# A Conformer and mixture-of-experts layer: the residual in token layout, the first norm by diagonal matrices, modulation rows spread through DRAM

## What is computed

```python
mod = silu(c) @ ada_w + ada_b
sh1, sc1, g1, sh2, sc2, g2 = split(mod, 6)
h = rmsnorm(x, mix_norm_g) * (1 + sc1) + sh1
u = h @ pw1_w + pw1_b                      # 2048 columns
a, gt = split(u, 2);  u = a * sigmoid(gt)
u = causal_depthwise_conv(u, dw_w, dw_b)   # 31 taps
u = silu(layernorm(u, ln_g, ln_b))
x = x + g1 * (u @ pw2_w + pw2_b)
h = rmsnorm(x, ffn_norm_g) * (1 + sc2) + sh2
logits = h @ router_w + router_b           # 32 experts, the best 4 of each token
gate = softmax(top 4 logits)
x = x + g2 * sum over the 4 of gate * expert(h)   # 1024 -> 2048, clamped SwiGLU, 1024 -> 1024
out = rmsnorm(x, final_norm_g)
```

## Time and profile before

| what | value |
|---|---|
| median of 3 runs | 1175.99 us (1170.95 to 1177.86) |
| the profiled execution's own time | 1175.84 us |
| its span, first to last instruction | 1174.0 us |
| TensorE busy | 994.6 us (85%) |
| VectorE busy | 354.4 us (30%) |
| ScalarE busy | 163.5 us (14%) |
| read from HBM | 455.79 MB, 389 GB/s over the span |
| TensorE's mean granted clock | 0.942 |

### The profile page before, as it was taken

One profiled execution on the slowest core, in us unless ns is written; L12 is line 12 of the kernel. 1 busy time (PEld: TensorE's weight loads), 2 busy tenths in 40 slices (PEclk: granted clock), 3 DMA queues, 4 the chain that ended last, 5 costly groups with the idle time before them and its releaser, 6 DMA issues.

```text
span 1174.0 us, 21008 instructions
## 1 busy us (share of the span) xinstructions
PE 994.6 (85%) x7636; PEld 468.4 (40%) x7637; DVE 354.4 (30%) x952; ACT 163.5 (14%) x360; POOL 8.1 (1%) x21
## 2 busy tenths in 40 slices
PE   5999988898999787999887999887899887878755
PEld 3776663334443333444323344323444322332322
DVE  3788555221222222132222123212112322222222
ACT  2333252101001101011110011010111010101002
POOL 1000000000000000000000000000000000000000
PEclk9999997998989998989998989998989989898978
DMA  9985964999999999999999999999999999999995
GB/s 356 285 346 190 392 247 172 420 421 421 422 372 424 422 422 422 421 392 424 422 422 422 422 417 399 421 422 421 423 421 392 422 422 422 422 422 422 422 421 228
DMA packets 84441, 457.24 MB, mean 389 GB/s; under 512 B 9183, under 2 KB 29783, under 8 KB 30622
## 3 DMA queue, kind: packets, MB, share of 16 engines
q1 hardware_dynamic: 83088, 456.16, 95.6%
q10 hardware_dynamic: 1326, 0.71, 0.2%
HBM read 455.79 MB, written 1.05 MB: 389 GB/s over the span
## 4 chain that ended last, share of the span: by engine, by line
PE 52%; DMA 34%; SPq 5%; DVE 4%; issue 3%; ACT 1%; ACTq 1%; POOL 0%; DVEq 0%; POOLq 0%
DMA ring<-in_exp_w 34%; PE bank L1252 22%; PE bank L1275 11%; PE bank L1124 5%; SPq L298 5%; PE bank L1145 2%; PE bank L1231 2%; PE bank L1072 2%; PE bank L1108 1%; PE bank L1219 1%; PE bank L1229 1%; PE bank L1262 1%; PE bank L1243 1%; DVE scratch L904 1%; PE bank L1054 1%
## 5 line engine op out<-in xcount | busy, mean ns | idle before, releaser
L1252 PE MATMUL bank<-ring,xg 128*32 128x256 f32 (+2 forms) x3200 | 443.8, 481 | 58.9 <-DMA ring<-in_exp_w 58.4
L1252 PEld LDWEIGHTS bank<-ring,xg 128*32 128x32 f32 (+2 forms) x3200 | 168.0, 129 | 320.7 <-issue 175.6
L1275 PE MATMUL bank<-ring,actT 128*32 128x512 f32 (+2 forms) x1056 | 217.2, 615 | 22.7 <-DMA ring<-in_exp_w 14.6
L531 ACT ACTIVATE act<-scratch 128x128 f32<-128x128 f32 (+2 forms) x66 | 25.6, 388 | 766.3 <-DVE scratch L904 764.9
L1275 PEld LDWEIGHTS bank<-ring,actT 128*32 128x32 f32 (+2 forms) x1056 | 75.5, 133 | 140.4 <-issue 109.0
L904 DVE TENSOR_SCALAR scratch<-bank 128x128 f32<-128x128 f32 (+2 forms) x66 | 25.3, 384 | 312.6 <-PE bank L1252 312.6
L893 DVE SCALAR_TENSOR_TENSOR acc<-bank,gate,acc 128x512 f32<-128x512 f32 x136 | 93.0, 743 | 54.7 <-PE bank L1231 45.4
L923 DVE TENSOR_TENSOR ysb<-bank,g2half 128x512 f32<-128x512 f32 x29 | 20.1, 692 | 219.0 <-PE bank L1275 219.0
L1219 PEld LDWEIGHTS bank<-onehot_bf,arena 128*128 128x128 bf16 x1632 | 57.4, 102 | 23.0 <-issue 23.0
L1231 PE MATMUL bank<-ysb,onehotT 64*128 64x512 f32 x240 | 60.4, 615 | 2.9 <-DVE ysb L923 2.1
L1219 PE MATMUL bank<-onehot_bf,arena 128*128 128x32 bf16 (+2 forms) x1632 | 61.0, 195 | 1.0 <-DVE arena L833 1.0
(11 more groups left out here) (222 smaller groups left out, 515.2 us busy)
## 6 DMA issues: line engine op xcount, KB each, us to landing
ring<-in_exp_w SPq DMA_DIRECT2D x396, 1024.0 KB, 24.1
ring<-in_ada_w SPq DMA_DIRECT2D x24, 1024.0 KB, 10.2
ring<-in_conf_pw_w SPq DMA_DIRECT2D x12, 1024.0 KB, 11.9
acc<-in_x SPq DMA_DIRECT2D x1, 1024.0 KB, 4.9
out<-acc SPq DMA_DIRECT2D x2, 512.0 KB, 3.1
g2full<-in_ada_b SPq DMA_DIRECT2D x1, 512.0 KB, 4.3
xT<-in_final_norm_g ACTq DMA_DIRECT2D x1, 512.0 KB, 3.7
b1f<-in_exp_b SPq DMA_DIRECT2D x1, 256.0 KB, 3.7
```

What stands on the lines that cost most here:

```text
L531: a.activation(act[:, h * c:(h + 1) * c], g_lim[h][:, 0:c], ACT.Sigmoid, scale=ALPHA).then_inc(sig_ready, 1)
L1252: ins = mm(up_to(m, n, r), xg[:, b, k, 0:m], wk[:, at:at + span(m)], start=False, stop=(k == KT - 1))
L1275: ins = mm(dst, actT[:, f % (2 * q), at:at + m], wk[:, f % 2 * D + r * H:f % 2 * D + (r + 1) * H], start=(f < sides), stop=(f >= KT - sides))
```

## The change

- The residual stays in `acc`, tokens as rows, all the way; `xT`, the turns of x2 and of h, and `pick` go.
- First norm: ScalarE sums the squares of each row, VectorE scales the identity by 1/rms of each token into two diagonal matrices, and x is turned by a product with them.
- Modulation columns: the stream begins with four chunks that hold only the scale columns (two blocks of 128 rows in each), then the first pw1 tile, then four chunks of shift columns, then the other pw1 tiles. Tile 0 is multiplied with scaled columns that have no shift yet; its bias is corrected by shift times weight, which TensorE makes as a row and turns in the middle of tile 1.
- pw2 goes with tokens as rows and 1024 outputs in two halves: token tile 0 over all channels, then the halves of token tile 1; a chunk holds 256 rows of pw2_w in pieces of 4 KB.
- g1, sh2, the second scale times norm gain (`a2_row`), g2 and g1 times the bias of pw2 are needed as rows on all 128 partitions. Each is stored to a DRAM scratch (`keep`) and read back into all partitions (`spread`). The first three spreads stand ahead of expert 0 on SyncE's queue, the last two behind its eighth chunk.
- Router: its weights are scaled by a2 and multiplied with turned x2, the shift's logits are one row (`log_row`), the norm is applied to the logits. Second norm: sums of squares by ScalarE in halves.
- Token tile 0 is routed and split while tile 1 is in work. The splitting of the expert biases moves in part to ScalarE; GpSimd no longer splits. `g2full` comes from DRAM; `ysb` and `gate4` are prepared behind the selection. The 13 transfers of convolution weights are issued behind the scale row. Rows of `ada_b`, `ffn_g` and `pw2_b` are loaded in 12 pieces with the small tensors, behind the twelfth chunk.

The core of the diff:

```diff
-    stream = [("ada", k) for k in range(KT)]
-    for t in range(KT):
+    stream = [("scale", q) for q in range(4)] + [("pw1", 0)] + [("shift", q) for q in range(4)]
+    for t in range(1, KT):
...
+                    two = slice(2 * k * P, (2 * k + 2) * P)
+                    src = (pw2_w[0, two, :] if what == "pw2" else
+                           ada_w[0, two, D:2 * D] if what == "scale" else ada_w[0, two, 0:D]
+                           ).rearrange("(a p) n -> p a n", p=P)
...
+            def keep(g):
+                sp.dma_start(mod_rows[g][0:2 * D].rearrange("(j n) -> j n", j=4),
+                             modrow[g][bass.ds(0, 4, 32), :]).then_inc(s_kept, 16)
+            def spread(to, g, at, landing):
+                sp.dma_start(to, mod_rows[g][at:at + D].partition_broadcast(P)).then_inc(landing, 16)
+            sp.wait_ge(s_row, 3)
+            keep(0)
+            sp.wait_ge(s_gbias, 1)
+            sp.dma_start(mod_rows[0][2 * D:3 * D].rearrange("(j n) -> j n", j=2),
+                         gbias_row[bass.ds(0, 2, 32), :]).then_inc(s_kept, 16)
+            sp.wait_ge(s_kept, 32)
+            spread(g1_row, 0, 0, s_rows1)
+            spread(xb_row, 0, 2 * D, s_rows1)
+            spread(sh2_row, 0, D, s_rows1)
...
+                    if first and q == KT - 1:
+                        sp.wait_ge(s_row, 4)
+                        keep(1)
+                        sp.wait_ge(s_kept, 48)
+                        spread(a2_row, 1, 0, s_rows2)
+                        spread(g2full[:, :], 1, D, s_rows2)
+            expert(0, 0, True)
...
+            a.wait_ge(p_c, 1)
+            a.activation(cact[:, :], bank[1][:, 0:KT], ACT.Silu).then_inc(s_cact, 1)
+            a.wait_ge(s_x, 16)
+            for t in range(TT):
+                a.activation(flat[:, t * D:(t + 1) * D], acc[:, t, :], ACT.Square,
+                             accum_out=ssq[:, t:t + 1]).then_inc(s_sq, 1)
+            a.wait_ge(s_const_v, 1)
+            a.wait_ge(s_sq, TT)
+            a.activation(fin[:, :], ssq[:, :], ACT.Sqrt, scale=1.0 / D, bias=eps[:, 0:1]).then_inc(s_fr0, 1)
+            a.wait_ge(p_vec, 1)
+            a.activation(vcol[:, :], bank[0][:, 0:VECS], ACT.Copy).then_inc(v_vec, 1)
+            a.wait_ge(used, number["scale", 3] + 1)
+            a.activation(modrow[0], bank[7][:, :], ACT.Copy).then_inc(s_row, 1)
...
+            a.wait_ge(p_sh, 1)
+            a.activation(modrow[1], bank[7][:, :], ACT.Copy).then_inc(s_row, 1)
+            a.wait_ge(used, number["shift", 3] + 1)
+            a.activation(crow, bank[0][:, T:2 * T], ACT.Copy).then_inc(s_crow, 1)
...
+                if t == 0:
+                    a.wait_ge(s_fix, 1)
...
+            squared(0, 0)
+            squared(0, 1)
+            rooted(0)
+            x2T_out(0, 0, 5)
+            x2T_out(0, 1, 6)
+            high(0, 0)
+            high(0, 1)
+            mid(0, 0)
+            mid(0, 1)
+            squared(1, 0)
+            x2T_out(1, 0, 1)
+            squared(1, 1)
+            rooted(1)
+            x2T_out(1, 1, 2)
+            high(1, 0)
+            high(1, 1)
...
+            v.wait_ge(s_fr0, 1)
+            link(v.reciprocal(frstd[:, :], fin[:, :]))
+            for t in range(TT):
+                v.tensor_scalar(diag[:, t, :], ident[:, :], frstd[:, t:t + 1], None, ALU.mult).then_inc(s_diag, 1)
...
+                v.tensor_scalar(hT[:, k, :], normed(k), a1[:, k:k + 1], None, ALU.mult).then_inc(s_h, 1)
...
+            v.wait_ge(p_row, 2)
+            column(sh1, P + KT, AB)
+            v.wait_ge(s_mod, 2)
+            v.tensor_copy(sh1wide, sh1[:, :].unsqueeze(2).to_broadcast([P, KT, 32])).then_inc(s_sw, 1)
+            v.wait_ge(p_t0, 1)
+            for k in range(KT):
+                v.tensor_scalar(hT[:, k, :], normed(k), a1[:, k:k + 1], sh1[:, k:k + 1],
...
+            v.wait_ge(p_corr, 1)
+            v.tensor_tensor(vcol[:, bass.ds(PB1, 2, 8)], bank[0][:, P + 16:P + 18], vcol[:, bass.ds(PB1, 2, 8)],
+                            ALU.add).then_inc(s_fix, 1)
+            v.wait_ge(s_fix, 1)
...
+            v.wait_ge(s_ab, 16 * 12)
+            v.wait_ge(used, number["ada", 2 * KT - 1] + 1)
+            v.tensor_tensor(modrow[0], bank[6][:, :], ada_rows[0], ALU.add).then_inc(s_row, 1)
...
+            v.tensor_tensor(gbias_row, modrow[0][0:64, :], pw2b_row, ALU.mult).then_inc(s_gbias, 1)
+            v.wait_ge(used, number["ada", 3 * KT - 1] + 1)
+            link(v.tensor_tensor(modrow[1], bank[7][:, :], ada_rows[1], ALU.add))
+            v.scalar_tensor_tensor(out=modrow[1][0:64, :], in0=modrow[1][0:64, :], scalar=1.0, in1=ffng_row[:, :],
+                                   op0=ALU.add, op1=ALU.mult).then_inc(s_row, 1)
...
+            v.wait_ge(s_rows1, 48)
+            for t in range(TT):
+                step(v.tensor_tensor(acc[:, t, :], acc[:, t, :], xb_row, ALU.add))
...
+            v.wait_ge(p_lrow, 1)
+            link(v.tensor_tensor(log_row[:, :], bank[0][:, 3 * P:3 * P + E], rb_row[:, :], ALU.add))
...
+            v.wait_ge(p_y, 1)
+            done = [gated_y(0, r) for r in range(2)]
             for r in range(2):
+                residual(0, r, done[r])
+            v.wait_ge(s_rows2, 32)
+            for r in range(2):
+                scaled(0, r)
+            base(0)
+            normed2(0)
+            for r in range(2):
+                modulated(0, r)
+            for r in range(2):
+                rest_of(0, r)
+            v.wait_ge(p_y, 2)
+            residual(1, 0, gated_y(1, 0))
+            scaled(1, 0)
+            logits(0)
+            choose(0)
+            for r in range(2):
+                low(0, r)
             for r in range(2):
                 step(v.tensor_copy(g2half[64 * r:64 * r + 64, :], g2full[64 * r:64 * r + 64, r * H:(r + 1) * H]))
+            base(1)
+            v.wait_ge(used, CH_EXP)
+            residual(1, 1, gated_y(1, 1))
+            scaled(1, 1)
+            normed2(1)
+            modulated(1, 0)
+            modulated(1, 1)
+            logits(1)
+            choose(1)
+            rest_of(1, 0)
...
+            low(1, 0)
+            low(1, 1)
+            step(v.scalar_tensor_tensor(out=key[:, :], in0=counts, scalar=float(E), in1=tie[:, :],
+                                        op0=ALU.mult, op1=ALU.add))
+            step(v.tensor_scalar(over[:, :], counts, float(WIDE), None, ALU.is_gt))
+            step(v.tensor_scalar(over2[:, :], counts, float(WIDE + SMALL), None, ALU.is_gt))
+            v.wait_ge(s_b2, 32)
+            v.tensor_tensor(ysb[:, 0, :], b2f[:, :], g2half[:, :], ALU.mult).then_inc(y_ready, 1)
+            step(v.memset(gate4, 0.0))
...
+            half_row("scale", 0).then_inc(used, 1)
+            pe.wait_ge(s_diag, TT)
             for k in range(KT):
                 for t in range(TT):
...
+                    ins = mm(bank[3 + k // 2][:, (k % 2) * T + t * P:(k % 2) * T + (t + 1) * P],
+                             acc[:, t, k * P:(k + 1) * P], diag[:, t, :], start=True, stop=True)
+            ins.then_inc(p_x, 1)
...
+            pe.wait_ge(*chunk_in(number["pw1", 0]))
+            pw1_half(0, 0)
+            pw1_half(0, 1).then_inc(p_t0, 1)
+            for q in range(4):
+                ins = half_row("shift", q)
+            ins.then_inc(p_sh, 1)
...
+                if t == 1:
+                    pe.wait_ge(s_crow, 1)
+                    for h in range(2):
+                        ins = mm(bank[0][:, P + 16 + h:P + 17 + h], crow[:, h * P:(h + 1) * P], sel1[:, :],
+                                 start=True, stop=True)
+                    ins.then_inc(p_corr, 1)
+                pw1_half(t, 1).then_inc(used, 1)
+                taps(t - 1)
...
+            for k in range(KT):
+                if k % 2 == 0:
+                    pe.wait_ge(*chunk_in(number["pw2", k // 2]))
+                pe.wait_ge(s_silu, k + 1)
+                if k == 4:
+                    pe.wait_ge(s_row, 4)
+                    for g in range(2):
+                        for q in range(4):
+                            at = T + 16 * g + 4 * q
+                            ins = mm(bank[0][:, at:at + 4], modrow[g][:, q * P:(q + 1) * P], ident[:, bass.ds(0, 4, 32)],
+                                     start=True, stop=True)
+                    ins.then_inc(p_row, 1)
+                for r in range(2):
+                    ins = pw2(0, r, k)
+            ins.then_inc(p_y, 1)
+            for k in range(KT):
+                ins = pw2(1, 0, k)
+            ins.then_inc(p_y, 1)
+            pe.wait_ge(s_sh2w, 1)
+            for k in range(KT):
+                ins = mm(bank[0][:, 3 * P:3 * P + E], sh2wide[:, k, :], rw[:, k, :], start=(k == 0), stop=(k == KT - 1))
+            ins.then_inc(p_lrow, 1)
+            turn_x2(0, 0, 5)
+            turn_x2(0, 1, 6)
             for k in range(4):
...
+                ins = pw2(1, 1, k)
+                if k % 2:
+                    ins.then_inc(used, 1)
+            pe.wait_ge(s_arw, 1)
+            route(0)
```

(47 more changed lines are left out.)

537 lines of the change are left out of this document (217 added, 320 removed).

## The result

The changed kernel takes 1186.58 us in the median of 4 runs (1184.90 to 1190.61), the kernel before 1174.62 in its 4 beside them: a ratio of 1.0099, 95% interval 1.0070 to 1.0129. It is 12 us slower; the forecast was 1185, 9.4 slower. Executions of one kernel lie some 3 to 10 us apart. The profiled execution took 1187.33 for a span of 1185.6, 11.6 longer than the one before.

A forecast was written before the change was run, and what follows sets the result against it. The span was taken as the weight ring's release after routing plus a stretch set by transfers. Release at 202.95 less 1.6 of front is 9.4 us later than 191.98; 1176.0 + 9.4 = 1185.4, rounded 1185, range 1171 to 1191.

The forecast's parts named there:

- rival A: Second rows through DRAM wait on SyncE's queue behind eight expert chunks; 1185, own range 1180 to 1191, chance 0.60.
- front: Work up to the first convolution taps, with new norm and chunk order: 1.6 us gained, bounds 0 and 3.5.
- second rows landed: The last two spreads land at 166.3, behind pw2 chunks, first store, three spreads, eight expert chunks and second store.
- stop of VectorE: VectorE, done with tile 0's x2 rows, stands from 155.0 to 166.3 until a2_row lands.
- rows to gather: From the second rows' landing at 166.3, through norm, pw2's end, logits and selection, to the gather at 191.3.
- gather to release: From first gather to the weight ring's release: 10.6 before, 11.65 with instructions moved behind the gather's start.
- the clock of 0.50: After some 12 us idle, TensorE's clock halves in pw2's last half; last products end at 180.0, against 177.1 unharmed.
- first taps near 44.6: Sign confirming the front: the first convolution taps start at 44.6 instead of 46.19.
- the queue is served in order: On SyncE's queue a small transfer gets no lane of its own; inferred from a router bias load taking 4.6 us.
- rival B: Second rows arrive by 155.0, so VectorE never stops; release 3.7 earlier, 1172, chance 0.26.
- the term of 1.05: Extra us between gather and release for table key, counts, ysb and gate4 clearing, partly hidden; between 0 and 1.31.
- Rival C: Front gets longer as late convolution-weight transfers delay the first taps to 48.6; 2.4 lost, 1189, chance 0.14.

The follow-up runs named there:

- e3: The changed kernel with the store and last two spreads on SyncE's queue behind five chunks of expert 0 instead of eight; 1178.54 us, ratio 1.0035.
- e1: The changed kernel with the second store and all five spreads moved ahead of the first expert's chunks; 1175.15 us, ratio 0.9997.
- h1: The changed kernel with 38 unread products keeping TensorE at work in its pause ahead of the first router product; 1185.82 us, ratio 1.0081.
- k1: The changed kernel with unread products, 13 ahead of the fourth shift chunk and 16 ahead of the first taps; 1188.96 us, ratio 1.0117.
- f1: The changed kernel with tile 0's corrected bias turned ahead of tile 1's product, not in its middle; 1183.60 us in 4 runs, ratio 1.0101.
- g3: e1 plus VectorE starting token tile 0 before the router logit row, and TensorE turning that tile inside pw2's second block; 1171.69 us, ratio 0.9966.
- e2: The changed kernel with the second store and its two spreads issued by ScalarE's queue, the store also earlier in time; 1175.92 us, ratio 1.0009.
- k3: g3 with tile 0's corrected bias turned ahead of tile 1 instead of in its middle; 1171.53 us, ratio 0.9970.
- k2: g3 with unread products, 13 ahead of the fourth shift chunk and 16 ahead of the first taps; 1172.13 us, ratio 0.9977.
- k4: k3 with unread products, 13 ahead of the fourth shift chunk and 4 ahead of the bias turn; 1170.53 us, ratio 0.9959.

## Why the prediction came out nearly right, and where it didn't

The forecast named rival A, and A is what happened: 1185 against 1186.58. The size is in part luck: both ends of its sum were off and cancelled in part. In the clock of the kernel before, that is with the measured 4.13 of the front taken off the times of after (LN sum at 119.32 against 115.19):

| step | forecast | measured |
|---|---|---|
| front | 1.6 gained | 4.13 lost |
| turn of the rows, logit row | 1.9 each | 1.84, 1.87 |
| x2 rows of tile 0 | 155.0 | 153.8 |
| second rows landed | 166.3 | 164.5 |
| stop of VectorE | 11.3 | 10.70 |
| rows to gather | 25.0 | 23.74 |
| gather to release | 11.65 | 10.77 |
| release, against 191.98 | 9.4 later | 11.15 later |

Of the signs that it named, the stop of VectorE and what ends it, the clock of 0.50, and an end that moves with the release all came; first taps near 44.6 did not (48.68).

- **The rows through DRAM: right in mechanism.** The forecast's "the queue is served in order" rested on one small transfer; the place of the store's packets behind the chunks and e3 show it. e1 shows that it is the whole net loss. It also gives the times that rival B forecast for rows in time: no slower than before, though not its 1172 (1175.15 measured). In e1's profile the LN sum is 2.45 late where B had its front 1.6 early, and the tables are 2.4 ahead of the kernel before, of which the span keeps 0.8. B itself did not happen in the changed kernel. The landing was 1.8 early: the chunks ran beside the spreads from the start, where the sum had put them behind. The sum also gave the first store 1.9 us behind its chunks and the second 0.7, without a reason; in the trace the chunks' stream ebbs at 162.0 and the answer is there at 162.91.
- **The clock: right.** Last pw2 used at 180.0 by forecast, 177.1 measured: 1.8 of the difference from the earlier rows, 0.4 from a shorter VectorE and 0.7 from faster work of TensorE. The products took 5.57, between the 3.6 of full speed and the 7.2 that half speed would give (an estimate, twice 3.6). h1 prices the slow clock at 1.6.
- **Gather to release: the term of 1.05 was mis-sized.** The moved instructions hid almost wholly behind the gather; 0.17 remained. Rows to gather was 1.3 too long, by the 0.4 and 0.7 just named and 0.15 behind them.
- **The front: this step failed, with its sign.** "Gain of the front: 1.6 us. Bounds: 0 ... 3.5": 4.13 lost lies outside. The last shift chunk was used at 32.77, not landed at 31.3; that is 1.5 with no margin ahead. The larger part is what the step left out: it priced every product of the front at full clock, and the clock fell to 0.50 from 37 to 39 and again from 50 to 53. k1 puts that share at about 3 of the 3.9 by which tile 2 is late (52.84 against 49.8), and the single pieces give the same: 0.87 in the correction, 0.69 in the first half of tile 1, 1.43 in the taps. Before, TensorE's pauses between the modulation at 22.66 and the taps add up to 1.0 us (0.72 and 0.30), and the clock stays at 1.00. That the clock could fall was used in the sum for the rows, and not looked for in the front, where the change puts new pauses.
- **Rival C** gave nearly the measured start of the first taps (48.6 against 48.68), by another mechanism: TensorE turned the convolution weights at 33.76 straight behind the chunk, without a wait for their landing. C did not happen, though it was near: ScalarE's queue still moved 13 packets between 32 and 33. The number agrees by chance.

What stays open: how much of the time, rather than of one profile, the front's clock costs, since k1's filling was too long and its time went the other way; why the clock falls at these places in one execution and not in another; and whether another queue would have saved a store issued behind the chunks. Few runs hide differences of 2 us: the front varies (tile 2 between 51.1 and 54.7 in the unfilled profiles with tile 0 ahead of its shift), and so does the stretch behind the tables, which lasts from 979.4 us (f1) to 985.1 (e3) in the fourteen profiles, though no change touches it.

## What to carry to other kernels

A short round trip through DRAM costs what stands ahead of it in its queue: ahead of a small store that something waits for, count the bytes issued before it on the same queue, and issue it first. (Another engine's queue was tried only with the store ahead of the chunks in time as well.) A change that puts a pause on TensorE has two prices, the pause and the slower work behind it; look for the second wherever the new order makes TensorE wait, not only at the large stop. When a total comes out right, compare it term by term: here errors of -4.0 and +5.7 stood behind a miss of 1.7.

## What the runs showed of the hardware

- Pauses of 1.80, 2.15 and even 1.14 us were followed by a granted clock of 0.50 for 3 to 10 us, but not in every execution: behind the 2.15 ahead of the taps it fell in the changed kernel, h1, e3 and g3, not in e1 and e2; behind the two short pauses (0.81 and 1.14) ahead of tile 0 it fell in h1, e3, g3 and k3, not in the changed kernel. A long pause is not even needed: in e3, h1 and k3 TensorE did not wait for the fourth shift chunk, and the clock was 0.50 from 39 to 41 all the same, behind chunk products with 32 columns of weights, turns and a pause of 0.59. So the pauses are not shown to be the cause. With the pauses filled (one profile each of k1, k2, k4) it was 1.00 from 28 to 56 us. The column shows 1.00 at the very start too, where the first 8 chunk products of the changed kernel take 1.94, against 1.06 later: there the duration is the better witness, and the start is slow before as well (16 mean products in 6.43, against 3.62 for 16 such products at 157.29).
- A row spread to 128 partitions lands later in company (3.8 to 5.3 us for the last two in the changed kernel, issued at 163): in e1 the five spreads took from 5.1 (the first pair) to 9.3 us (the last). The transfers issued from 130 to 150 us in e1 (KB each, median us to landing):

```profile
xg<-mod_rows SPq DMA_DIRECT2D x2, 512.0 KB, 5.1
ffn_rows<-mod_rows SPq DMA_DIRECT2D x2, 512.0 KB, 7.6
g2full<-mod_rows SPq DMA_DIRECT2D x1, 512.0 KB, 9.3
```
- A 128x128 float32 product took 0.244 us with its two passes when issued back to back (3.17/13 in k1), and 0.23 in h1's longer row: a filling has to be counted by that.
